# Splitting the last products of each stage into 320 and 192 tokens

## The reference

```
x = x + rms_norm(mix, g_mix_post[l])
...
ca = memory_cross_attention(h, m, w_mem_q[l], w_mem_kv[l], w_mem_o[l])
x = x + rms_norm(ca, g_mem_post[l])
h = rms_norm(x, g_ffn_pre[l])
x = x + rms_norm(swiglu(h, w_gate_up[l], w_down[l]), g_ffn_post[l])
```

## Time and profile before

| | us |
|---|---|
| three runs | 2176.84 median, 2168.41 to 2179.32 |
| the profiled execution, its own time | 2168.62 |
| its span, first to last instruction | 2166.8 |
| TensorE busy in the span | 2091.8 (97%) |
| VectorE, ScalarE, POOL busy | 1108.0, 875.5, 973.6 |
| mean granted TensorE clock | 0.992 of full |

### The profile page before, as it was taken

One profiled execution on the slowest core, in us unless ns is written; L12 is line 12 of the kernel. 1 busy time (PEld: TensorE's weight loads), 2 busy tenths in 40 slices (PEclk: granted clock), 3 DMA queues, 4 the chain that ended last, 5 costly groups with the idle time before them and its releaser, 6 DMA issues.

```text
span 2166.8 us, 27220 instructions
## 1 busy us (share of the span) xinstructions
PE 2091.8 (97%) x9546; PEld 1669.9 (77%) x9546; DVE 1108.0 (51%) x1670; ACT 875.5 (40%) x1442; POOL 973.6 (45%) x489
## 2 busy tenths in 40 slices
PE   8999899989999999999999999999999999999997
PEld 5777787877888888787767788888777777888886
DVE  3535834234577776763473543434575426434345
ACT  5226864345222222533474422222465544323232
POOL 3437875434455444433234344444435633444443
PEclk9999999999999999999999999999999999999999
DMA  5440052204466664363003233333222022333332
GB/s 180 167 142 12 20 194 88 78 30 149 143 232 213 229 235 136 96 253 126 20 1 102 64 95 96 96 97 96 87 79 68 1 68 66 95 95 95 97 97 86
DMA packets 66768, 234.38 MB, mean 108 GB/s; under 512 B 7169, under 2 KB 8577, under 8 KB 66561
## 3 DMA queue, kind: packets, MB, share of 16 engines
q1 hardware_dynamic: 66688, 233.33, 32.7%
HBM read 231.20 MB, written 2.10 MB: 108 GB/s over the span
## 4 chain that ended last, share of the span: by engine, by line
PE 79%; issue 6%; DVE 5%; ACT 4%; POOL 4%; DMA 1%; SPq 0%; POOLq 0%; DVEq 0%; ACTq 0%
PE bank L781 24%; PE bank L783 24%; PE bank L782 24%; PE bank L892 2%; POOL WL L663 2%; PE bank L877 1%; POOL sq L695 1%; PE bank L959 1%; DVE acc L1997 1%; POOL t L695 1%; DVE Y L2268 0%; DVE bank L2070 0%; PE bank L1285 0%; DMA stage<-panels 0%; ACT sq L1416 0%
## 5 line engine op out<-in xcount | busy, mean ns | idle before, releaser
L663 POOL TENSOR_TENSOR WL<-stage,WH 128x1024 fp32r<-128x1024 f32 x272 | 675.5, 2484 | 954.0 <-ACT WH L1388 953.9
L1388 ACT ACTIVATE WH<-stage 128x1024 fp32r<-128x1024 f32 x272 | 288.3, 1060 | 897.5 <-PE bank L783 850.7
L781 PE MATMUL bank<-H,WH 128*128 128x512 f32 x1324 | 520.2, 393 | 20.5 <-POOL WL L663 7.5
L782 PE MATMUL bank<-H,WH 128*128 128x512 f32 x1324 | 518.2, 391 | 0.0
L783 PE MATMUL bank<-H,WL 128*128 128x512 f32 x1324 | 517.8, 391 | 0.0
L781 PEld LDWEIGHTS bank<-H,WH 128*128 128x128 f32 x1324 | 250.2, 189 | 78.5 <-issue 17.6
L782 PEld LDWEIGHTS bank<-H,WH 128*128 128x128 f32 x1324 | 250.4, 189 | 52.5 <-issue 0.5
L783 PEld LDWEIGHTS bank<-H,WL 128*128 128x128 f32 x1324 | 250.3, 189 | 52.5
L2268 DVE TENSOR_TENSOR Y<-bank,Y 128x512 f32<-128x512 f32 x344 | 226.4, 684 | 99.6 <-PE bank L783 98.5
L782 PE MATMUL bank<-HID,WH 128*128 128x512 f32 x688 | 267.6, 389 | 0.0
L783 PE MATMUL bank<-HID,WL 128*128 128x512 f32 x688 | 267.6, 389 | 0.0
(11 more groups left out here) (396 smaller groups left out, 3084.0 us busy)
## 6 DMA issues: line engine op xcount, KB each, us to landing
stage<-panels SPq DMA_DIRECT2D x296, 512.0 KB, 3.5
ahead<-ada SPq DMA_DIRECT2D x96, 512.0 KB, 5.2
RAW<-panels SPq DMA_DIRECT2D x18, 512.0 KB, 3.9
apiece<-ada SPq DMA_DIRECT2D x16, 512.0 KB, 3.7
x<-xT SPq DMA_DIRECT2D x3, 1024.0 KB, 7.7
outT<-x SPq DMA_DIRECT2D x8, 256.0 KB, 2.0
x<-xT SPq DMA_DIRECT2D x2, 512.0 KB, 4.2
Y<-bias SPq DMA_DIRECT2D x1, 1024.0 KB, 6.2
```

The costliest lines, as they stand in the source:

```text
L663: pool.tensor_tensor(low_of(p, slot), stage[:, slot, :], high_of(p, slot).bitcast(F32), ALU.subtract).then_inc(s_split, 1)
L781: pe.matmul(out, wh, rh, start=start, stop=False)
L782: pe.matmul(out, wh, rl, start=False, stop=False)
L1388: act.activation(high_of(p, slot), stage[:, slot, :], ACT.Copy).then_inc(s_hisplit, 1)
```

## The change

The tokens are cut into a first part of 320 (`COLS[0]`) and a second of 192 (`COLS[1]`) for the last products of each of the six stages.

- **Projections.** Chunks 0 to 3 stay whole. Chunks 4 to 7 are multiplied for the first part, and then again for the second (`last_chunks`), so their weights are loaded into the array twice. Panels 4 and 5 go into a new tile `WD`.
- **Feed-forwards.** The `down` of the last two groups becomes one step (`last_downs`): for each chunk the products of both groups go into one bank, 12 matmuls, for all 8 chunks of the first part and then of the second. It needs the four panels of both groups and starts after the activation of the last group. The host orders these four panels to suit; two of them lie in `WD`. Three banks are used in turn.
- **Norm and residual.** The sums and the root of the first part (`half_sums`, `half_root`) stand behind the first chunk of the second part; VectorE scales and adds the first part (`first_half`) between its work on the second. ScalarE squares the first part's new `x`, and POOL now adds these squares (`first_half_squares`), with the split of the next stage's first panel between its additions 5 and 6. The second part follows as before, at 192 columns (`second_half`); the last root is made for all 512 tokens.
- `warm` goes from 6 + 16 + 14 matmuls at a boundary to 12 + 14. The output leaves in 16 transfers and not 8.

```
+            def last_chunks(name):
+                for half in range(2):
+                    for c in range(4, KC):
+                        p, turn = p0 + c, 4 * half + c - 4
+                        if not half:
+                            pe.wait_ge(s_split, p + 1)
+                        if turn >= 2:
+                            freed(pe, proj, turn + 3)
+                        for k in range(KC):
+                            last = three(T[turn % 2][:, COLS[half]], ...)
+                            if half and c == 4 and k == 3:
+                                half_sums(name, 0)
...
+                def last_downs():
+                    p0, groups_before = ff_down(name, groups - 2), groups - 2
+                    pe.wait_ge(sm["split"], 2 * groups)
+                    for half in range(2):
+                        for m in range(KC):
+                            turn, part, at, cols = 8 * half + m, m // 4, m % 4 * P, COLS[half]
+                            if not half and m % 4 == 0:
+                                pe.wait_ge(s_split, p0 + 2 * part + 2)
+                            pe.wait_ge(sm["added"], 4 + 8 * groups_before + max(turn - 2, 0))
...
                 if groups % 2 == 0:
                     up(groups - 1, 1)
-                    down(groups - 2, 0)
-                down(groups - 1, (groups - 1) % 2, True)
+                last_downs()
...
+            def sums_after(name):
+                half_sums(name, 1)
+                warm(G[1], 12)
+                pe.wait_ge(s_log, upto(LOG, name, 1))
+                pe.wait_ge(s_padd, (KC - 1) * (AFTER.index(after) + 1))
+                pe.matmul(ST[:, COLS[0]], ones, acc[:, COLS[0]], start=True, stop=True).then_inc(s_sum, 1)
+                for m in range(KC):
+                    pe.wait_ge(s_sq, upto(SQ, after, 1, m))
+                    pe.matmul(ST[:, COLS[1]], ones, sq[:, m % 2, COLS[1]], ...).then_inc(s_sum, 1)
+                warm(G[1], 14)
...
+            def boundary(name, p0):
+                first_half_squares(name, 1, 6)
+                split_low(p0, 0)
+                first_half_squares(name, 6, KC)
+                residual(name)
+                split_low(p0 + 1, 1)
...
                     for j in range(2):
+                        if last and (j or not gated):
+                            act.wait_ge(s_used, p + j * per + 1)
+                            if j == (1 if gated else 0):
+                                panel_high(p0, 0)
...
                         act.activation(t[:, j, :], banks[2 * j][:, :], ACT.Silu if gated else ACT.Relu)
+                        if last and j:
+                            panel_high(p0 + 1, 1)
...
+                panel_high(p0 + 2, 0)
                 for m in range(KC):
+                    first_squares(m)
+                    if m == 2:
+                        panel_high(p0 + 3, 1)
...
+                half_root(name, 1)
+                act.wait_ge(s_used, p0 + 4)
+                if after:
+                    panel_high(p0 + 4, 0)
+                    for m in range(5, KC):
+                        square_after(name, 0, m)
+                    square_after(name, 1, 0)
+                    square_after(name, 1, 1)
+                    panel_high(p0 + 5, 1)
+                    for m in range(2, KC):
+                        square_after(name, 1, m)
```

More of the change, by code:

```diff
@@ L108, with squares_order @@
 POOL_ADDS = (1, 3, 5)
+HALVED = {"ca": ("mem_o", "x_ffn"), "ffn": (None, "x_a"), "a": ("a_out", "x_mlp0"), "mlp0": (None, "x_b"),
+          "b": ("b_out", "x_mlp1"), "mlp1": (None, None)}
+AFTER = [_x for _, _x in HALVED.values() if _x]
+COLS = [slice(0, 5 * S // 8), slice(5 * S // 8, S)]
+PROJ_A = {"mem_o": 0, "a_out": 4, "b_out": 20}
+def squares_order():
+    order = []
+    for name, n, _ in STATS:
+        if name in HALVED:
+            proj, after = HALVED[name]
+            whole = 4 if proj else 0
+            order += [(name, None, m) for m in range(whole)] + [(name, 0, m) for m in range(whole, KC)]
+            mixed = "y4 x0 x1 y5 x2 x3 x4 y6 x5 x6 y7 x7" if proj else "y0 y1 y2 x0 y3 x1 y4 x2 y5 x3 y6 x4 y7 x5 x6 x7"
+            for kind, m in mixed.split():
+                if kind == "y":
+                    order.append((name, 1, int(m)))
+                elif after:
+                    order.append((after, 0, int(m)))
+        elif name in AFTER:
+            order += [(name, 1, m) for m in range(KC)]
+        else:
+            order += [(name, None, m) for m in range(n)]
+    return order
@@ new lines, in first_of, with upto, whole_or @@
+def first_of(table, name):
+    return [key[0] for key in table].index(name)
+def upto(table, *key):
+    return table.index(key) + 1
+def whole_or(name, half, m):
+    return None if HALVED[name][0] and m < 4 else half
+LAST_DOWN = {PANEL0[_name] + _groups * (6 if _gated else 4) - 4: _name for _name, _groups, _gated in FFNS}
+IN_WD = {}
+for _at in LAST_DOWN:
+    IN_WD[_at], IN_WD[_at + 1] = 0, 1
+for _proj, _ in HALVED.values():
+    if _proj:
+        IN_WD[PANEL0[_proj] + 4], IN_WD[PANEL0[_proj] + 5] = 0, 1
@@ L301, in squares_total @@
                 return acc
-            return G[1] if name in ("ffn", "mlp0", "mlp1") else O[0]
+            return G[1] if name in ff else O[0]
         def residual_in(name, m):
@@ L1463, in evacuate_high, with half_square @@
                         after(c)
-            def evacuate_squares(name, stat_name):
-                for c in range(KC):
-                    used(PANEL0[name] + c, c % 2)
-                    square(stat_name, c, G[c % 2][:, :])
-                    act.activation(Y[:, c, :], G[c % 2][:, :], ACT.Copy).then_inc(s_free, 1)
-                    if name == "a_out" and c == 3:
+            def half_square(name, half, m, source):
+                cols = slice(0, S) if half is None else COLS[half]
+                if (name, half, m) == SQ[first_of(SQ, name)]:
+                    act.wait_ge(s_sum, first_of(SUM, name))
+                if m >= 2:
+                    held = max(m - 2, 1)
+                    act.wait_ge(s_add, upto(ADD, name, whole_or(name, half, held), held))
+                act.activation(sq[:, m % 2, cols], source, ACT.Square).then_inc(s_sq, 1)
@@ L1974, in _ @@
             feed_forward(*FFNS[2])
-            root("mlp1")
         @block.vector
```

494 lines of the change are left out of this document (357 added, 137 removed).

## The result

| | before | after |
|---|---|---|
| median, us | 2174.8 (2168.4 to 2179.3, 4 runs) | 2232.4 (2225.5 to 2233.6, 4 runs) |
| ratio | | 1.026, 95% interval 1.0225 to 1.0295 |
| the profiled execution, its own time | 2168.6 | 2225.5 |
| its span | 2166.8 | 2223.7 |
| TensorE busy | 2091.8 (97%) | 2106.1 (95%) |

What follows compares the result with a forecast made beforehand. It took TensorE to bound the kernel except some 110 us of boundaries. Feed-forwards 12.1 + 9.6 + 6.9, projections 3.1 and clock 5 gave +37 us on 2168.6, thus 2205.6, and 2209 us as median; range 2182 to 2229.

Steps and rivals of the forecast that it cites:

- The pitches: Cut products on TensorE: 0.147 us each at 320 columns, 0.118 at 192; a pair costs 0.265 and replaces 0.2266.
- The first wait: Feed-forwards, behind the last up product: TensorE waits 4.8 us in mlp0 and mlp1, 2.3 in ffn.
- The second: Feed-forwards, at chunk 4 of the first part: TensorE waits 3.4 us for panel p0 + 3 in each.
- mlp0's tail: Behind mlp0's last product: 2.7 us to the second root, 6.2 for squares with POOL's split, then 5.5 and 4.3.
- the one in which the side engines hide entirely: Faster rival, all boundaries: TensorE alone sets the time, -1.8 us in each of six, 2161 us; chance 0.08.
- the one of POOL's split: Rival at the boundaries: only POOL's split between the squares hides, +13 us, 2185 us; chance 0.13.
- One bound: Cut products at 192 columns: with the continued slope, 0.093 us, the cut would cost 7 us in all.
- the tail behind the last product: Boundaries, last product to next stage's first: 18 to 19 us in ffn and mlp0, 15 behind projections.
- the clock: TensorE behind the new waits: the lower granted clock adds 5 us (none to 15).
- The tail of the projections: Behind projections: POOL's last additions end at 32.3, sums at 37.0, next product at 41.4 against 40.9 before; +0.5 each.
- The worse rival: Behind most waits the clock stays at 1.2 GHz: 15 instances cost 25 us instead of 5, 2229 us; chance 0.11.
- the base: Profiled execution's 2168.6 us is 8.2 under the runs' median; half of that was added, giving 2209 us.

Runs made afterwards that it cites:

- e2: Changed kernel with ScalarE copying panels p0 + 1 (mlp0, mlp1) and p0 + 3 (all feed-forwards) earlier: 2208.3 us, 1.0168 of before.
- e3: Changed kernel with POOL splitting the next stage's first panel behind its additions (not mlp0), ScalarE's extra panel copies moved later: 2227.5 us, 1.0247 of before.
- e6: Changed kernel with ScalarE's squares of the first part's new x waiting for one POOL addition less: 2231.3 us, 1.0263 of before.
- g1: Changed kernel with TensorE's new waits filled by useless matmuls and ScalarE's squares waiting for one addition less: 2217.6 us, 1.0191 of before.
- g3: Changed kernel with 5 matmuls of warm and not 12 ahead of a boundary's last sums: 2230.9 us, 1.0256 of before.
- e1: Changed kernel with TensorE's new waits filled with matmuls without use: 2225.6 us, 1.0258 of before.
- e7: Changed kernel with ScalarE taking the second part's chunk 7 ahead of the squares of x chunks 5 and 6 in projections: 2232.0 us, 1.0269 of before.
- f2: Changed kernel with only projections halved, 256 and 256, POOL's split last, weaker wait of squares, chunk 7 first: 2172.9 us, 0.9999 of before.
- f4: Changed kernel, all six at 256 and 256, early panels, weaker wait, chunk 7 first, POOL's split last (not mlp0), residual by VectorE: 2185.1 us, 1.0058 of before.
- e8: Changed kernel with early panels, POOL's split last, waits filled, weaker wait and chunk 7 first together: 2206.4 us, 1.0158 of before.

## Why the prediction came out so

**Right, in direction and in most of the mechanism.** The pitches: 0.147 us at 320 columns, 0.112 at 192 (0.118 forecast), so the second part took 11.8 us (12.4). The first wait: 4.77 us in mlp0 and mlp1, 2.46 in ffn (4.8 and 2.3). The second: 3.16 (3.4). Who ends them is shown by e2. Of mlp0's tail the forecast had 2.7 to the root, 6.2 for the squares with POOL's split, 9.8 from there to the product; measured were 3.6, 7.15 and 11.0. Of the rivals, the one in which the side engines hide entirely is far off. In the one of POOL's split, e3 leaves the loss at 2.5%: the split was one of several things at the end. One bound was added up wrongly: at a pitch of 0.093 for 192 columns the cut costs 7.7 us in six boundaries and not 7.

**Wrong: the size, by 20 us of span.** The table of lengths shows where: 13 us in the feed-forwards, 8 in the projections, and the rest of the stretches lost 4 where 5 had been set down as clock for everything. Two terms of the sum were too small: the tail behind the last product, 15.7 us in the five boundaries that have a next stage, and the clock, some 7 us (the other stretches' 4 are taken as clock here). The second parts, 0.6 us shorter each than forecast, hide nearly 4 us of that.

*The tail of the projections.* "ScalarE squares chunk 5 only at 27 ... at 32.3; second residual, squares and sums until 37.0; 4.4 to the product: 41.4." In b the square of chunk 5 came at 27.2 and VectorE was through at 27.9 (27.7 forecast), but POOL's last addition ended at 33.5 and the sums at 40.0. The forecast costed the squares by POOL's 0.86 us and ScalarE's own; in the trace a chunk takes the hand-over's 1.57 us. So the tail of 14.9 us that the forecast had was 18.1 (and the 18 to 19 us of ffn and mlp0 were 21.7). e6 and g1 show it: with the weaker wait the tails shrink by 2.2 us, two thirds of the 3.2 that were missing, and in e6's b POOL ends at 31.4, the sums at 36.5 and the boundary at 41.8, beside the forecast's 32.3, 37.0 and 41.4. The remaining third lies elsewhere in each. In b it is the `warm` at the lower clock: POOL ended at 1837.11 and the sums began at 1838.97. In ca the sums began 0.6 us behind POOL, but the product came 5.2 us behind them and not 4.4, since ScalarE waited 1.1 us for a panel's transfer ahead of `H`. g3 shows that leaving warms out gives nothing back: the sums themselves then run at the lower clock.

*The clock.* "I add 5 us (none to 15)." It lies mostly inside the feed-forwards: products behind the two waits took 1.5 us more than in e1 in ffn and in mlp0, and 4.7 in mlp1, 7.7 together. Of the 4.0 us of the other stretches 3.1 lie between mlp0's boundary and b, where the granted clock was 0.97 and 0.95 in stretches in which before had 1.00 and 0.97. What filling gives back was measured in two ways. e1 against the changed kernel: 6.8 us by the medians, 7.6 by the lengths. g1 against e6: 13.6 us by the medians, since e6 has the lower clock behind the wait at the fifth chunk too. The same code differs there between executions and even within one: 48 products take 7.1 us in mlp0 of the profiled execution of after, 9.7 in its mlp1, and 9.8 to 9.9 in mlp0 of e6 and e7. The worse rival, with all 15 waits at half rate for 25 us, put its result at 2229; its number is nearer than the forecast's, but its reason isn't the one: e1 leaves 50 of the 57 us with the clock nearly restored.

Against the median 2 us more come from the base: I had taken the runs' median 4.1 us above the profiled execution, and it is 6.2. That both profiled executions had the full clock in the first stretch, as only three of 17 did, fits this; of the other runs no trace shows it.

**Not settled.** In the feed-forwards 13 us were missing, and the clock explains some 7.6 (e1). Most of the rest is the tail, 3.0 us longer than forecast in ffn and mlp0: in mlp0 the root came 0.9 us later, the squares' hand-over took 1 us more, and the last stretch 1.2 us more, with a granted clock of 0.50 and 0.59 in its sums. Why the root was late is open, and e6 shortens these tails by only 0.6 and 0.9 us. Why the clock falls behind a wait in one execution and not in another is open too.

**Where the gain went.** The change hides a part of 10.5 us of residual and sums at a boundary. The projections show what that is worth when everything else is repaired: from 2.3 us won (ca in f2) to 2.0 lost (a). In ca the tail is 4.4 us shorter and the cut costs 2.1; in a the wait for panel 6 and the clock behind it take 4.4 more. In a feed-forward, the price is that no product is left to run beside the last activation, which no repair brought below 2.5 to 3 us, and that the clock falls behind this wait where nothing fills it. The tail is no gain in mlp0 (20.3 us in f4, 19.5 before) and 2.9 us in f4's ffn.

## What to carry to other kernels

Work put beside products is only hidden if each in-order engine gets through its whole list in that time: add up the hand-overs (here 1.57 us a chunk) and not the instructions. Before merging the last steps of a pipeline, ask which product then covers the last stage's activation. And a repair of a wait of 2 us may show nothing in the time, since the clock takes it back; look at the length of the stretch itself, and hold the clock in a second run. Size a filling by the wait that is left: once another repair has removed the wait, the filling is the loss (e8). And try each repair without each of the others: e7's order took back all that e6 had won.

## What the runs showed of the hardware

- The same subtraction of 128x512 on VectorE took 0.69 us with POOL idle (e2), 1.12 beside the end of a POOL instruction, and 2.42 when POOL's 2.34 us ran beside it; in both of the latter it ended 0.55 us after POOL. The forecast had used this, and here it has its undisturbed value. By the Trainium skill (SBUF — State Buffer, Who interferes with whom) a VectorE instruction with two SBUF inputs contends with a GpSimd instruction that reads SBUF, and the one that comes second blocks until the first is done. The runs agree: POOL's had started first in both.
- A narrow matmul of 192 columns with a weight load of 128 has a pitch of 0.112 us, hardly more than the 0.11 of 128 columns.
- The granted clock behind the same wait of 3.2 us was 1.00 in one execution (after, mlp0) and 0.50 to 0.60 for some 5 us in another (e6, mlp0). 48 products of 320 columns took 7.1 us in the one and 9.8 in the other, and 9.7 in mlp1 of the first execution itself.
- In code that no edit touched, the first 485 us of the kernel, executions differ by up to 10 us; from 100 to 200 us their granted clock was 0.93 to 1.00.
